# Second layer's second MLP product: token columns taken in two halves of 192

## What is computed

```
def sq_relu_mlp(h, w1, w2):
    return jnp.square(jax.nn.relu(h @ w1)) @ w2
...
        h = rms_norm(x, p['norm_w'][li, 1]) * (1 + sc2) + sh2
        x = x + g2 * sq_relu_mlp(h, p['w_mlp1'][li], p['w_mlp2'][li])
```

## Time and profile before

| | before |
|---|---|
| median of 2 runs | 1048.97 us (1048.93 to 1049.0) |
| span of the profiled execution | 1047.8 us; the profile lists no other time of its own |
| PE busy | 1020.6 us, 97% |
| PEld busy | 941.7 us, 90% |
| DVE / ACT / POOL busy | 568.5 / 486.1 / 140.8 us |
| chain that ended last, PE's share | 92% |

### The profile page before, as it was taken

The page is one execution under the profiler, slowest core; times in us unless marked ns, Lnnn a source line. Parts: engine busy times, 40 slices in busy tenths (PEclk is TensorE's granted clock), DMA queues, the critical chain, the costliest instruction groups (busy, mean ns, idle before and its releaser), DMA issues.

```text
span 1047.8 us, 17863 instructions
## 1 busy us (share of the span) xinstructions
PE 1020.6 (97%) x7330; PEld 941.7 (90%) x7330; DVE 568.5 (54%) x914; ACT 486.1 (46%) x858; POOL 140.8 (13%) x173
## 2 busy tenths in 40 slices
PE   6999999999999999999999999999999999999997
PEld 3888885778999999999997989886999999999997
DVE  5556676564744345354457576576465445345452
ACT  5544665664553342342344556667464234252342
POOL 0162200011010010110110342350001011010110
PEclk9999999999999999999999999998999999999999
DMA  9987719645435445445445532223223524333311
GB/s 330 343 283 244 237 48 322 202 162 195 152 121 167 155 161 161 161 159 162 153 129 186 176 104 68 86 87 101 80 81 121 162 92 149 120 120 120 121 41 61
DMA packets 156974, 160.44 MB, mean 153 GB/s; under 512 B 3146, under 2 KB 155108, under 8 KB 156900
## 3 DMA queue, kind: packets, MB, share of 16 engines
q1 hardware_dynamic: 154512, 156.15, 45.0%
q0 software_dynamic: 704, 1.97, 0.6%
q10 hardware_dynamic: 1684, 1.26, 0.4%
HBM read 156.09 MB, written 3.28 MB: 152 GB/s over the span
## 4 chain that ended last, share of the span: by engine, by line
PE 92%; DVE 3%; ACT 2%; issue 1%; DMA 1%; SPq 0%; DVEq 0%; ACTq 0%
PE G L585 63%; PE G L590 13%; PE OB L607 4%; PE TB L554 4%; PE SC L918 2%; PE OB L932 1%; PE SC L694 1%; DMA raw<-in_w_ada 1%; PE OB L715 1%; PE OB L785 1%; PE TB L900 1%; ACT wH L1024 1%; PE SC L670 1%; PE SC L664 1%; PE SC L626 1%
## 5 line engine op out<-in xcount | busy, mean ns | idle before, releaser
L585 PE MATMUL G<-opH,wH 128*128 128x386 f32 (+1 forms) x768 | 267.7, 349 | 1.1 <-DVE wL L1505 0.8
L1024 ACT ACTIVATE wH<-raw 128x2048 fp32r<-128x2048 f32 x94 | 179.6, 1911 | 180.9 <-PE G L585 178.1
L585 PE MATMUL G<-opH,wL 128*128 128x386 f32 (+1 forms) x768 | 260.4, 339 | 0.0
L585 PE MATMUL G<-opL,wH 128*128 128x386 f32 (+1 forms) x768 | 260.2, 339 | 0.0
L1505 DVE TENSOR_TENSOR wL<-raw,wH 128x2048 fp32r<-128x2048 f32 x94 | 215.8, 2296 | 42.9 <-ACT wH L1024 42.9
L585 PE MATMUL G<-hidH,wH 128*128 128x384 f32 x512 | 173.3, 338 | 0.0
L585 PE MATMUL G<-hidH,wL 128*128 128x384 f32 x512 | 172.1, 336 | 0.0
L585 PE MATMUL G<-hidL,wH 128*128 128x384 f32 x512 | 172.1, 336 | 0.0
L585 PEld LDWEIGHTS G<-opH,wH 128*128 128x128 f32 x768 | 144.9, 189 | 9.8 <-issue 5.4
L585 PEld LDWEIGHTS G<-opL,wH 128*128 128x128 f32 x768 | 144.8, 189 | 1.6
L585 PEld LDWEIGHTS G<-opH,wL 128*128 128x128 f32 x768 | 144.9, 189 | 0.0
(11 more groups left out here) (246 smaller groups left out, 1192.6 us busy)
## 6 DMA issues: line engine op xcount, KB each, us to landing
raw<-in_w_mlp SPq DMA_DIRECT2D x64, 1024.0 KB, 5.2
raw<-in_w_ada SPq DMA_DIRECT2D x48, 1024.0 KB, 7.0
raw<-in_w_in_even SPq DMA_DIRECT2D x13, 1024.0 KB, 7.2
raw<-in_w_in_odd SPq DMA_DIRECT2D x12, 1024.0 KB, 5.1
raw<-in_w_out_even SPq DMA_DIRECT2D x4, 1024.0 KB, 6.6
raw<-in_w_out_odd SPq DMA_DIRECT2D x4, 1024.0 KB, 5.0
xin<-in_x_sample SPq DMA_DIRECT2D x2, 512.0 KB, 5.7
out_y_sample<-yout SPq DMA_DIRECT2D x1, 768.0 KB, 4.1
```

The lines of the kernel that those rows point to most:

```text
L585: mm = pe.matmul(G[:, s, 512 * m:512 * m + cols], w[:, s, k, P * m:P * m + P], a[:, k, 0:cols], start=first and q == 0, stop=last and q == 2)
L1024: act.activation(wH[:, u % 2, :, :], raw[:, pos % RAW, :, :], ACT.Copy).then_inc(w_high, 1)
```

## The change

In the second layer, where the moving operand is `hidH` and `hidL`, every [128 x 384] area is filled in two halves of 192 tokens: the three passes over tokens 0 to 191, then the three passes over tokens 192 to 383. The weight block is the same for both halves. The flag `start` (it marks the first product into a PSUM area) goes with the first pass of the first half. All other products stay as they were.

```
+                token_parts = ((0, cols // 2), (cols // 2, cols)) if mH is hidH and u >= U_MLP1 else ((0, cols),)
...
                         for m in range(2):
-                            for q, (w, a) in enumerate(passes):
-                                mm = pe.matmul(G[:, s, 512 * m:512 * m + cols], w[:, s, k, P * m:P * m + P],
-                                               a[:, k, 0:cols], start=first and q == 0, stop=last and q == 2)
+                            for t0, t1 in token_parts:
+                                for q, (w, a) in enumerate(passes):
+                                    mm = pe.matmul(G[:, s, 512 * m + t0:512 * m + t1], w[:, s, k, P * m:P * m + P],
+                                                   a[:, k, t0:t1], start=first and q == 0 and t0 == 0,
+                                                   stop=last and q == 2, skip_group_check=True)
```

## The result

The changed kernel takes 1087.26 us (1086.88 to 1087.64) where the kernel before took 1048.97: 1.0366 times as long, 95% interval 1.0349 to 1.0383, or 38.3 us more. The forecast was 1087.1 us, in a range of 1076 to 1102.

The account below looks back on a forecast made before the run. PE was taken to bound the stage, with each half costing its weight load, 111.7 ns: 49.65 ns for each of 768 products, 38.1 us on 1048.97, gives 1087.1 us. The range was 1076 to 1102 us, 8 times in 10.

Parts of the forecast that it names:

- What binds: Second MLP's product: PE busy the whole time, DVE and ACT half or less, so each ns on PE goes into the time.
- The choice between streaming and load: For 192-column halves in the second MLP: streaming gives 179.6 ns a pair against 173.75; load's pace gives 111.7 ns a half.
- the bare load after a pause: At 657.07 and 1036.55 us the next load starts 0.11 us later; taken as the load's price for 128 columns.
- The 111.7 ns: Price taken for each half, from full float32 products that load 128 columns and follow at 2.01 us / 18.
- The slope of the load records: Load records: 64 columns more cost 53 ns, so 128 take about 106 ns; lower bound of a half, 29.4 us in all.
- the 117.8 ns of the 256-column product: Upper bound of a half's price: fewer columns with the same load should be no slower; 47.5 us in all.
- The line of streaming: Line through 384 and 256 moving columns: 0.437 ns a column plus 5.9 ns, giving 89.8 ns for 192.
- The sum: Second MLP: 2 x 111.7 - 173.75 = 49.65 ns for each of 768 products, 38.1 us.
- that rival: The load hides beneath the halves' streaming; only their fixed part remains: +4.5 us, 1053.5 us; chance 10%.
- The narrow product: Rival: 192-column products lose the fast type's pace, a pair taking 650 ns: +366 us, 1415 us; chance 6%.
- a lower clock: Rival: PE waits more for loads and its clock falls to 0.50, 1.2 GHz: +210 us, 1259 us; chance 2%.
- the signs to look for: Profile after: 24 products fill 2.68 us, 8098 loads and products, load 0.11 us ahead of its MATMUL, PE's waits near 2 us.

## Why the prediction was right

- **What binds.** PE had no slack in the stage, so its cost went into the time in full: 37.9 us of PE and 37.7 us of span. That nothing else was moved held too: the waits of PE after 787 us fell from 2.2 to 1.8 us.
- **The choice between streaming and load.** This was the step on which all hung, and the trace of before could decide it in spite of having no product of this shape: the bare load after a pause, 0.11 us, was the right price. The run with half of the weight columns shows that the forecast was right for this reason. The 111.7 ns came within 0.5 ns, and that is partly luck. The 18 and the 8 instructions there are not products but records, two for each full float32 product as in the earlier trace rows: `hg_out` (line 785) makes 9 products and `states` (line 763) 4. One record with its load does compare to one product of the reduced type. But 384 columns take 325 ns a record, so 128 columns would stream in some 108 (an estimate), and these records would stand near 111 ns apart without a word from the load. The slope of the load records, 106 ns, was 5 ns too low for a bound of the pace, the 117.8 ns of the 256-column product a bound with 6 ns to spare.
- **The line of streaming.** From two points, 384 and 256 columns, it gave 89.8 ns for 192 and 145.7 for 320. Measured: 89.0 with half of the weights, and 255.0 - 111 = 144 for 320. It was good within 2 ns at both.
- **The sum.** 49.65 ns x 768 = 38.1 us; 49.8 ns by the chain's long piece, 38.3 us by the medians.
- **The rivals.** The load does not hide: the time of that rival, 1053.5 us, came only with the load halved (1052.95). Its sentence that no product of before takes less than 0.11 us holds for blocks of 128 columns alone: the records with 64 stationary columns on line 715 of the kernel before stand 67.5 ns apart, twelve in 0.81 us. The narrow product kept its pace down to 64 columns, as the starts there show. The stretch cited against a lower clock is not full of records at the load's pace: the 44 of them that it has fill some 5 of its 12.9 us. But the clock stayed at 1.00 where the halves run, as this stretch of the changed kernel shows (columns as in the earlier trace rows):

```profile
820.00:854.00 34.00, 34.00 (x281) 34.00 (x280) 11.06 (x15) 5.75 (x3) 0.00 (x0) 1.00 0.35 112
```

- **What was wrong in it.** Of the signs to look for, one failed. I wrote that a load would start 0.11 us ahead of its MATMUL and the next load with the MATMUL. It is 0.09 and 0.02. I had taken the MATMUL's start for the end of its load. In the earlier trace rows the two come within 0.01 us of each other (657.29 and 657.30) only because 256 columns stream in 117.8 ns, about as long as a load takes; the earlier trace rows already spoke against it, with a MATMUL that starts 0.03 us behind its load (1036.55 and 1036.58). The distance from load to load was right, the picture of who waits where in the record was not.

## What to carry to other kernels

In this kernel a product has two prices, the streaming of its moving columns and the load of its stationary block, and costs the longer of them. With 128 stationary columns of the reduced float32 type at full clock the load is 111 ns. By the line of streaming the two are equal at (111 - 5.9) / 0.437, some 240 moving columns; that is an estimate, as no run lies between 192 and 256. Cutting a wide product into narrower ones costs a few ns a piece until a piece goes below that, and each piece below it costs a full load: so it was at 192, 128 and 64 columns. Neither the order of the loops nor the same block twice running took a load away. A block of half the columns made the load shorter, at half the output. Whether a kernel written with one load for several products would pay it once was not tried.

The number of columns alone does not give the load. The transposes of the changed kernel also load 128 columns, with records of 141 ns in place of 188 to 192:

```profile
L554 PEld LDWEIGHTS TB<-ident,xT 128*128 128x128 f32 x24 | 2.5, 141 | 2.3 <-ACT yout L1482 2.3
```

## What the runs showed that I had not expected

PE's record hides a wait for weights. The changed kernel spends 22 of each 111 ns waiting for a block that isn't there yet (111.25 less the 89.0 of the run with half the load), and its profile says PE is busy for 34.00 of 34.00 us, with no idle time ahead of any product and no wait in the list. PEld's share doesn't tell either: it was busy for all of the stretch before the change too, when the load had 60 ns to spare, because a load record of 188 ns is some 77 ns longer than the 111 from one load to the next, so records overlap. The Trainium skill, "Perfetto Trace Analysis", section "Identifying the Most-Contended Engine", prefers the sum of the LDWEIGHTS records over the window, beside the share of peak FLOPs, to the busy share of the matmuls. Here that sum is over the whole of the window both times, 188 of each 173.75 ns before and 192 of each 111.25 after: it rises, but does not mark where the load begins to bind. What tells is the distance from load to load: 174 ns means streaming, 111 means loading. The other sign is the length of a MATMUL record of the same shape, 274 ns with a wait in it and 251 to 253 without.

The price of the wide product also surprised me: the 173.75 ns of a 384-column product stay (174.6 by 4.19 / 24) with half a load beneath, though by the line 5.9 ns of them do not go with the columns.
